# Modulation quarters summed in two alternating banks, and the index key as one piece behind the last quarter

## The reference

```
mod = silu(c) @ w_ada + b_ada                 # 2048 x 6144: shift, scale, gate
h = rms_norm(x, g_norm) * (1 + scale) + shift
proj = h @ w_in                               # qa ka va za | q_idx k_idx w_idx | qb kb vb zb
k_idx = rms_norm(k_idx, k_norm_idx)           # 64 columns; w_idx has 16
qa = rms_norm per head of 128; ka likewise
logits = q_idx . k_idx -> relu -> weighted sum over 16 index heads -> top 64 keys per query
```

## Time and profile before

| | |
|---|---|
| three runs | 1988.01, 1993.59, 1994.17 us; median 1993.59 |
| profiled execution | 1993.05 us, span 1991.3 us |
| PE busy | 1892.2 us, 95% of the span |
| POOL, DVE, ACT busy | 67%, 46%, 41% |
| DMA | 352.60 MB, mean 177 GB/s |

### The profile page before, as it was taken

The page is one execution under the profiler, slowest core; times in us unless marked ns, Lnnn a source line. Parts: engine busy times, 40 slices in busy tenths (PEclk is TensorE's granted clock), DMA queues, the critical chain, the costliest instruction groups (busy, mean ns, idle before and its releaser), DMA issues.

```text
span 1991.3 us, 32274 instructions
## 1 busy us (share of the span) xinstructions
PE 1892.2 (95%) x12975; PEld 1582.5 (79%) x12975; DVE 906.2 (46%) x1122; ACT 809.2 (41%) x1095; POOL 1325.3 (67%) x683
## 2 busy tenths in 40 slices
PE   5889999999989899998999999999999999999997
PEld 2668878888657798887789877888888888888886
DVE  1004647560351324565644361654455555733223
ACT  3224444444444454333422444434334343433333
POOL 2448878888239489962543496798888888844442
PEclk8899999999999999999999999999999999999999
DMA  9984545555765356543100145455555555555553
GB/s 328 363 306 164 176 168 175 189 187 190 283 223 180 112 163 212 191 147 127 46 25 4 48 167 176 162 190 189 181 181 187 190 190 180 182 196 197 194 190 127
DMA packets 174433, 352.60 MB, mean 177 GB/s; under 512 B 6735, under 2 KB 19421, under 8 KB 171773
## 3 DMA queue, kind: packets, MB, share of 16 engines
q1 hardware_dynamic: 173437, 346.94, 52.4%
q10 hardware_dynamic: 896, 4.20, 0.6%
HBM read 349.02 MB, written 2.10 MB: 176 GB/s over the span
## 4 chain that ended last, share of the span: by engine, by line
PE 59%; POOL 20%; issue 18%; DVE 2%; ACT 1%; POOLq 0%; DVEq 0%; ACTq 0%
PE bank L919 21%; POOL WL L547 19%; PE bank L921 10%; PE bank L873 6%; PE bank L874 6%; PE bank L875 6%; PE bank L1265 5%; PE bank L1185 1%; PE bank L1195 1%; PE bank L1228 1%; PE bank L395 0%; PE bank L1154 0%; POOL HX L840 0%; POOLq L546 0%; POOL arena L814 0%
## 5 line engine op out<-in xcount | busy, mean ns | idle before, releaser
L547 POOL TENSOR_TENSOR WL<-WR,WH 128x1024 fp32r<-128x1024 f32 (+2 forms) x516 | 1229.4, 2393 | 487.1 <-ACT WH L1478 485.6
L1478 ACT ACTIVATE WH<-WR 128x1024 fp32r<-128x1024 f32 (+2 forms) x560 | 577.4, 1037 | 813.3 <-PE bank L875 450.3
L919 PE MATMUL bank<-HX,WH 128*128 128x512 f32 x1840 | 649.6, 398 | 6.9 <-POOL WL L547 5.2
L921 PE MATMUL bank<-HX,WL 128*128 128x256 f32 x1840 | 515.4, 280 | 0.0
L919 PEld LDWEIGHTS bank<-HX,WH 128*128 128x128 f32 x1840 | 345.6, 188 | 92.5 <-issue 5.9
L873 PE MATMUL bank<-WH,HX 128*128 128x512 f32 (+2 forms) x864 | 339.1, 393 | 12.3 <-POOL WL L547 7.3
L921 PEld LDWEIGHTS bank<-HX,WL 128*128 128x128 f32 x1840 | 347.2, 189 | 0.0
L875 PE MATMUL bank<-WH,HX 128*128 128x512 f32 (+2 forms) x864 | 331.5, 384 | 0.0
L874 PE MATMUL bank<-WL,HX 128*128 128x512 f32 (+2 forms) x864 | 331.3, 383 | 0.0
L873 PEld LDWEIGHTS bank<-WH,HX 128*128 128x128 f32 x864 | 163.0, 189 | 50.9 <-issue 14.0
L874 PEld LDWEIGHTS bank<-WL,HX 128*128 128x128 f32 x864 | 163.2, 189 | 31.1 <-issue 1.9
(11 more groups left out here) (295 smaller groups left out, 1957.9 us busy)
## 6 DMA issues: line engine op xcount, KB each, us to landing
WR<-in_w_in SPq DMA_DIRECT2D x96, 1024.0 KB, 5.0
WR<-in_ffn_w_gate SPq DMA_DIRECT2D x44, 1024.0 KB, 5.1
WR<-in_ffn_w_up SPq DMA_DIRECT2D x44, 1024.0 KB, 5.1
WR<-in_ffn_w_down SPq DMA_DIRECT2D x44, 1024.0 KB, 5.1
arena<-in_w_ada SPq DMA_DIRECT2D x64, 512.0 KB, 9.4
WR<-in_w_out SPq DMA_DIRECT2D x32, 1024.0 KB, 5.1
WR<-in_w_ada SPq DMA_DIRECT2D x16, 1024.0 KB, 5.1
WR<-in_w_in SPq DMA_DIRECT2D x12, 768.0 KB, 4.3
```

The lines of the kernel that those rows point to most:

```text
L547: eng.tensor_tensor(half(WL, n % NSLOT, *w), half(WR, n % NSLOT, *w), half(WH, nth(n) % 2, *w), ALU.subtract).then_inc(ready, 1)
L919: pe.matmul(bank[:, :].rearrange("p (h n) -> p h n", h=2), wh[:, k, o], HX[:, :, kk, :], start=kk == 0, stop=False, skip_group_check=True)
L921: last = pe.matmul(bank[:, 0:L], wl[:, k, o], HX[:, 0, kk, :], start=False, stop=kk == KT - 1, skip_group_check=True)
L1478: act.activation(half(WH, nth(n) % 2, *w), half(WR, n % NSLOT, *w), ACT.Copy).then_inc(hi_ready, 1)
```

## The change

- The key's column pieces, one in each quarter, become one piece of all 16 row tiles (128 columns, 1 MB) behind quarter 3's C, number n_kw = 12. The quarters have three pieces each. All later pieces have numbers lower by 3.
- The modulation sums of quarter q go to bank q % 2, and their first one waits for mod_ready of two quarters before. Their places are now three before I0, two before I1, three before C.
- SP's order: the last modulation load of each quarter is issued behind the I0 piece of that quarter.
- The key's product goes to bank 4 once its queries are copied. Turning it is done inside branch chunk 1, turning it back inside branch chunk 2, and the wait on kb_ready stands behind chunk 2.
- ACT's share of the key, with its wait for ki_var, stands between `high(n + 2)` and `high(n + 3)` of chunk 1. DVE's program has the same order as before.
- In the second layer the wait for y_sum stands before the load with slot 3, which is now the third piece of w_out_2 and was the fourth.

```diff
-        n_br = n_in + 3 * PIECES
+        n_kw = n_in + 3 * PIECES
+        n_br = n_kw + 1 - PIECES
...
-            ada_quarter(0, 4, 8)
+            ada_quarter(0, 4, 7)
             for q in range(4):
                 in_piece(q, 0)
+                ada_quarter(q, 7, 8)
+                if q < 3:
+                    ada_quarter(q + 1, 0, 2)
                 in_piece(q, 1)
                 if q < 3:
-                    ada_quarter(q + 1, 0, 3)
+                    ada_quarter(q + 1, 2, 4)
                 in_piece(q, 2)
                 if q < 3:
-                    ada_quarter(q + 1, 3, 5)
-                in_piece(q, 3)
-                if q < 3:
-                    ada_quarter(q + 1, 5, 8)
+                    ada_quarter(q + 1, 4, 7)
+            load(n_kw, w_in[:, KW_COL:KW_COL + P].rearrange("(k p) n -> p k n", p=P), P, KT)
...
-                elif m == 3:
+                elif m < 4 and (n_wo2 + m) % NSLOT == 3:
                     sp.wait_ge(y_sum, 1)
...
-                if i == 0 and n >= 8:
-                    pe.wait_ge(mod_ready, n // 8)
+                if i == 0 and n >= 16:
+                    pe.wait_ge(mod_ready, n // 8 - 1)
...
+            pe.wait_ge(act_took, 2)
+            piece(n_kw, 0, False, 4, P, KT)
+
+            def key_turn(kk):
+
+                if kk == 2:
+                    pe.wait_ge(kiT_taken, 1)
+                    pe.wait_ge(act_took, 4)
+                    for t in range(TT):
+                        last = pe.transpose(BANK[6][:, t * P:t * P + P], KIT[:, t * P:(t + 1) * P], ident[:])
+                    last.then_inc(ki_ready, 1)
...
+                    begin = {1: key_turn, 2: key_spread, 5: index_from(0), 6: index_from(8)}.get(j) if b == 0 else None
...
+            def take_key():
+
+                act.wait_ge(ki_ready, 1)
+                for t in range(TT):
+                    act.activation(KI[:, t, :], BANK[6][:, t * P:t * P + KW], ACT.Copy).then_inc(act_took, 1)
+                act.wait_ge(ki_var, 1)
+                sqrt_of(krstd, krstd).then_inc(ki_rstd, 1)
...
                     if b or j:
                         high(n + 2, more, **relus(0))
+                        if b == 0 and j < 3:
+                            (take_key, take_spread)[j - 1]()
                         high(n + 3, more, **relus(1))
...
-            dve.wait_ge(act_took, 2)
+            dve.wait_ge(act_took, 8)
```

More of the change, by code:

```diff
@@ L508, in width_of @@
         def width_of(n):
-            if n_in <= n < n_in + 4 * PIECES and n % 4 == 0:
+            if n == n_kw:
                 return P
@@ L518, in tiles_of @@
         def tiles_of(n):
-            return PK
+            return KT if n == n_kw else PK
         def nth(n):
@@ L731, in lows @@
                         low(first + q, i * PIECES)
-            lows(n_in, n_in + 4 * PIECES)
+            lows(n_in, n_kw)
+            low(n_kw)
             lows(n_br + PIECES, n_gate)
@@ L949, in mod_cols, with piece @@
                 for j in range(4):
-                    last = pe.matmul(BANK[0][:, 2 * j:2 * j + 2], mod_row[:, j * P:(j + 1) * P], half_col,
+                    last = pe.matmul(BANK[m % 2][:, 2 * j:2 * j + 2], mod_row[:, j * P:(j + 1) * P], half_col,
                                      start=True, stop=True)
                 last.then_inc(mod_cols_ready, 1)
-            def piece(n, q, token, first, width):
-                wh, wl = view(WH, nth(n) % 2, width), view(WL, n % NSLOT, width)
-                for k in range(PK):
+            def piece(n, q, token, first, width, pk=PK):
+                wh, wl = view(WH, nth(n) % 2, width, pk), view(WL, n % NSLOT, width, pk)
+                for k in range(pk):
                     kk = q * PK + k
@@ L960, in piece @@
                         pe.wait_ge(ht_ready, kk // 2 + 1)
-                    split(n, k)
+                    split(n, k, pk=pk)
                     if token:
@@ L972, in piece @@
                                            kk == 0 and f % 2 == 0, kk == KT - 1)
-                    done(k, last)
+                    done(k, last, pk)
             def to_feature(src, g, first, base, scaled=False):
@@ L1535, in _ @@
             for q in range(4):
+                high(n_in + 3 * q)
                 act.wait_ge(ada_done, 8 * (q + 1))
-                act.activation(mod_row, BANK[0][:, :], ACT.Copy).then_inc(row_took, 1)
-                high(n_in + 4 * q)
+                act.activation(mod_row, BANK[q % 2][:, :], ACT.Copy).then_inc(row_took, 1)
+                high(n_in + 3 * q + 1)
                 act.wait_ge(mod_ready, q + 1)
@@ L1542, in _ @@
                                    scale=gs[:, k:k + 1]).then_inc(x_scaled, 1)
[L1543 to L1551 removed]
+                high(n_in + 3 * q + 2)
             def take_queries(j):
[L1555 removed]
+                act.wait_ge(piece_done, n_in + 10 + j)
                 for t in range(TT):
@@ L1597, in _ @@
                             act.wait_ge(headT_ready, b * 4 + (j - 1))
+                        if b + j == 0:
+                            act.wait_ge(piece_done, n_kw)
+                            for t in range(TT):
+                                act.activation(stage[:, 0, t, :], BANK[2 + t][:, :], ACT.Copy).then_inc(act_took, 1)
+                            act.wait_ge(piece_done, n_kw + 1)
+                            act.activation(KIT, BANK[4][:, 0:L], ACT.Copy).then_inc(kiT_taken, 1)
+                            high(n_br + PIECES + 1)
+                            continue
                         read_chunk(n, pair, [stage[:, j % 2, t, :] for t in range(TT)], more=more)
```

59 lines of the change are left out of this document (22 added, 37 removed).

## The result

The changed kernel is slower: 2004.37 us median (2000.24 to 2006.31, 6 runs) beside 1986.96 (1979.41 to 1994.17, 6 runs) of the kernel before, ratio 1.0074, 95% interval [1.005, 1.0099]. Its profiled execution had 2006.31 us, span 2004.6, with 1.71 around it. That is 13.3 us more than the profiled execution before. A part of the experiments is about why.

A forecast was written before the change was run, and what follows sets the result against it. Loads were taken to set the pace up to about 140 us, PE behind that. The terms -5 + 1.0 + 0.9 + 5 + 2.7 = +4.6 on 1993.05 gave 1997.7 us, range 1988.5 to 2003.5.

The forecast's parts named there:

- The likeliest case: Whole kernel: measured time within 0.3%, 6 us, of no change; chance 0.51.
- Gain 5 at the start: Modulation quarters, up to the last mod_cols: load 31 lands sooner and PE's work shrinks; 5 us gained, ends 2.5 and 7.
- A KW piece at 1.5 us: Loads ahead of load 31: each key column piece costs 1.5 us, between 0.7 by bytes and 2.1 with the dip.
- +1.0 up to chunk 1: From mod_cols to branch chunk 1: waits and turns of 3.4 us go, 36 matmuls of 4.4 us are added; net +1.0.
- The wait of 2.77 stays: Before branch chunk 1: PE's 2.77 us wait for the split x stays, its chain over ACT and DVE being the same.
- +0.9 for the turns: Branch chunks 1 and 2: the key's turns now stand inside them, adding 0.3 + 0.6 = 0.9 us.
- +5 for the pause: Branch chunk 1: the head norm behind the key makes PE wait 2.9 to 7.3 us; middle taken, +5.
- Root at S + 16.7: Branch chunk 1, S being its start: ACT takes the first head's root at S + 16.7, before at S + 12.2.
- +2.7 for the clock: Behind the new pause of 5 us: PE runs at half clock, costing 2.7 us, or nothing if the pause is gone.
- One scaling at each border, and a small gain: Rival, branch chunk 1 and start: one scaling per POOL border, stall 7.3, clock 3.4, gain 3; +9.6, 2002.7 us; chance 0.22.
- The key chain: Rival, branch chunk 1: scalings find POOL idle and end ahead of the chunk, no stall; -3.1, 1990.0 us; chance 0.2.
- The y_sum wait: Second layer: the wait moves from the fourth load of w_out_2 to the third, and costs nothing.

The follow-up runs named there:

- second pair of profiles: The changed kernel and the kernel before, each run again unchanged: medians 2003.31 us and 1991.78 us, ratios to before 1.0064 and 0.9995.
- e2: The changed kernel, but ACT scales a quarter's x before it rounds the I1 piece: 1994.43 us, ratio 1.0031 to the kernel before.
- e4: The changed kernel with e2's edit and the first head norm ahead of the key in branch chunk 1: 1988.58 us, ratio 1.0001 to the kernel before.
- h2: g3 with ACT's root for the first head right behind the copy of the index key: 1979.26 us, ratio 0.996 to the kernel before.
- g3: e4 with the next quarter's mod_cols behind the first row tile of a quarter's C: 1984.49 us, ratio 0.996 to the kernel before.
- e3: The changed kernel with one DVE scaling in place of eight, for the first head alone: 1997.24 us, ratio 1.0044 to the kernel before.

## Why the prediction was right or wrong

The likeliest case, no change within 0.3%, did not come; slower by more than that had 0.38. The forecast was 1997.7 us with a range from 1988.5 to 2003.5, and the median of 2004.37 lies 0.9 above that range. Even so the time looks better than the forecast was. It started from 1993.05 us, and the median of six runs of the kernel before is 1986.96: a change of +4.6 was forecast, and the medians are 17.4 apart, the profiled executions 13.3, the traces at the third turn 9.7. That the time came as near as it did is in part the luck of a high starting point. By its own steps, for the traces shown ahead:

- **Gain 5 at the start: this step failed.** The end of the last mod_cols moved by 0.5 us, in the second pair of profiles by -2.8. The step took load 31 to land at 131.2 and PE to be waiting for it once the KW pieces were gone. It landed at 137.4, issued only at 129.22, when PE had got to the sum that frees its buffer, and PE did not wait. The step had priced loads and PE apart, and not ACT's list, in which the rounding of I1 had moved ahead of the scaling of x: 6.0 us of waits for the split x in quarters 0 to 2, where before there were none. I had read the same diff for chunk 1 and costed a wait behind a rounding there; at the start I wrote that the chain over ACT and DVE was the same. e2 put the scaling first, and then 131.2 and 138.7 were met within half a microsecond, in part by chance (next point); the last mod_cols of e4 and h2 ended at 140.7 and 138.3.
- **A KW piece at 1.5 us was too much.** The key's load in g3 has the queues to itself. Windows of 1 us:

```profile
142.00:143.00 1.00, 1.00 (x10) 1.00 (x10) 0.00 (x0) 0.07 (x1) 1.00 (x1) 1.00 1.14 345
143.00:144.00 1.00, 1.00 (x11) 1.00 (x10) 0.00 (x0) 0.99 (x1) 1.00 (x1) 1.00 1.18 311
```

  Rows of 512 bytes ran at 311 to 345 GB/s with the queues full, beside some 387 for rows of 2 KB: 0.8 us for 256 KB, near the 0.7 by bytes. The Trainium skill, page "DMA: Bandwidth & Descriptors", section Specifications, gives 512 bytes as the least transfer that runs at line rate. Beside the 387 GB/s of this case, the measurement is 11 to 20% short of that. The dip of the earlier trace rows was not the piece's. The changed kernel, with no such piece there, has one too, 0.69 at 191 GB/s from 72 to 75 us. And in the kernel before, SP had issued the KW piece at 57.32 and the next load only at 67.05, since it waited for PE to free a slot of WR (SP's waits from 55 to 75 us):

```profile
SPq L583 <- PE bank L875: 11.7, 2, 7.7
```

  The queues ran dry in the dip, and the piece landed at 68.9, some 0.7 us behind the load ahead of it. With 0.8 the step gives 133.3 for load 31; in e2, g3, e4 and h2, which have ACT's scaling first, PE's wait for it ended at 130.82, 132.33, 133.20 and 133.26.
- **+1.0 up to chunk 1** was +0.4 (28.1 in place of 27.7 us), with the wait for the split x longer by 1.02 and the rest shorter. "The wait of 2.77 stays" failed in every quarter.
- **+0.9 for the turns** was right, 0.3 in chunk 1 and 0.6 in chunk 2.
- **+5 for the pause** was 6.49, inside its ends of 2.9 and 7.3. Root at S + 16.7 was foreseen and measured, scalings "10 to 12.5" and 11.76, and POOL's halves came in a bunch. On the way there two errors made up for each other: the key's squares and mean took 4.6 us in place of 3.3, two squares being long at 1.52 and 2.07 us, and the head's squares, sums and mean took 3.7 in place of 4.5. For the pause itself the choice of the middle was off.
- **+2.7 for the clock** was 2.4: from the first head's turn to the second's 25.7 us in place of 22.7 (before 195.23 to 217.90, after 201.96 to 227.64), less the 0.6 of the key's turn.
- **Sum:** -0.5 + 0.4 + 0.9 + 6.5 + 2.4 = 9.7, the distance of the rows at 240.57 and 250.31. The error is 4.5 of the gain, 1.5 of the pause, less 0.9.
- **The rivals.** "One scaling at each border, and a small gain" was nearest (+9.6, 2002.7), by a way of its own: at the start its gain of 3 was not there, and the scalings took fewer borders than eight. The key chain did not hide. The Trainium skill's page "GPSIMD Engine Reference", section Specifications, which the prediction cites for this rival, has GpSimd contend with VectorE instructions in a two-port mode or with two SBUF inputs. The scalings have one such input, and no trace names their mode; they did get longer beside POOL. The Trainium skill's page "SBUF — State Buffer", section Terms, says more sharply what contention is: the port pair is held for a whole instruction and the loser is fully blocked. The casts of 0.42 and 1.45 us and the scalings of 5.98, 8.15, 11.76 and 15.81 us agree with it, as far as durations can.
- **The y_sum wait** cost nothing: no new wait of PE shows there.

What is left open: the median of the changed kernel lies 12 to 17 us above that of the kernel before, its traces 9.7 and 13.6 us at the third turn. Where the first pair of traces parts further, the second pair did not repeat it in full. The mean granted clock of the runs (0.977 beside 0.984) says that the changed kernel spends more time at half clock, a part of it in the first 200 us. How much of that it causes later, by moving later pauses, I cannot tell from one profile each.

## What to carry to other kernels

When an engine's list is written out by hand, a work item that waits for a load must not stand ahead of one that a critical chain needs. Read each engine's new list against the landing times, not only the engine that the change is meant for: here one swapped line on ACT took away 7 us of gain. Where loads wait for buffers that the slowed engine frees, the delay reaches the loads too (load 31 was issued 9 us later than in e2). A chain on an engine that a busy neighbour holds up, as POOL did DVE here, is priced by that neighbour's gaps, so it is cheapest to start it just before the neighbour has work (5.98 us in place of 15.82), and a pause that is removed at one place may come back a chunk later (e3). And small synchronizing matmuls belong inside a longer piece of work, whose rest then covers their consumers (g3).

## What was unexpected of the hardware

- At granted clock 1.00 the same loop of matmuls ran a whole stage at 346.7 ns or at 353.4 ns a pair. In one stage this differed between two executions of one kernel, for both kernels; over the longer stage it is 9 us, nearly the size of the change. The granted clock of the windows doesn't show it.
- Behind the same pause the half clock lasted 3.4, 6.8 or 10.2 us from one profile to another: near 575 us it was 3.4 and 10.2 us in the two executions of the kernel before. Behind 300 us, without the end of the kernel, they had 27 and 34 us of it; the changed kernel 41 and 34.
- Eight scalings of 128 x 128 on DVE took between 5.98 and 15.81 us, by what POOL did meanwhile.
